# Multi-head latent attention of a two-block transformer: one running sequence of steps over all heads, v computed ahead, the division moved to the output, and the projections of later pairs placed in three of eight steps

## The reference, cut to what matters

```python
up = (c_kv @ kv_w_up).reshape(B, T, MLA_HEADS, QK_NOPE + V_HEAD)   # 16 heads, 64 + 64
k_nope, v_sh = up[..., :QK_NOPE], up[..., QK_NOPE:]
c_q = rmsnorm(h @ q_w_down[j], q_norm_g[j])
q = (c_q @ q_w_up[j]).reshape(B, T, MLA_HEADS, QK_NOPE + QK_ROPE)  # 64 + 32
q_rope = apply_rope(q[..., QK_NOPE:], cos[:, None, :], sin[:, None, :])
...
s = jnp.einsum('bqhd,bkhd->bhqk', qn, k_nope) + jnp.einsum('bqhr,bkr->bhqk', qr, k_rope)
s = s.astype(jnp.float32) * scale
mask = k_chunk[None, :] <= q_chunk[:, None]          # chunks of 64
s = jnp.where(mask[None, None], s, NEG_INF)
p = jax.nn.softmax(s, axis=-1)
return jnp.einsum('bhqk,bkhd->bqhd', p.astype(v.dtype), v)
...
m = o.reshape(B, T, MLA_HEADS * V_HEAD) @ o_w[j]
```

## Time and profile before

| | us |
|---|---|
| median of 3 runs (lowest, highest) | 2600.51 (2596.22, 2605.82) |
| the profiled execution, its own time | 2600.76 |
| its span | 2599.0 |
| TensorE busy in the span | 2374.7 |
| VectorE, ScalarE busy | 1349.9, 970.5 |
| stretch of the phase `heads` | 1093.2 to about 1386 |

### The profile page before, as it was taken

How to read it: one execution, slowest core, us unless ns; L and a number is a source line. 1 busy time by engine, 2 the same in 40 slices (tenths; PEclk the granted TensorE clock), 3 DMA queues, 4 the chain that set the end, 5 groups by cost and what they waited for, 6 DMA issues and landing times.

```text
span 2599.0 us, 38262 instructions
## 1 busy us (share of the span) xinstructions
PE 2374.7 (91%) x14842; PEld 1767.0 (68%) x14842; DVE 1349.9 (52%) x2188; ACT 970.5 (37%) x1544; POOL 60.7 (2%) x84
## 2 busy tenths in 40 slices
PE   5989999968999997799989899999777999999998
PEld 3856666656888884555556688887544787788886
DVE  5566777654646465634442654544555433544443
ACT  4563333324423233434443542323334443422222
POOL 0001111100000000000000000000000000000000
PEclk8999999969999998866778999999866899999999
DMA  3200000012333321100011132322110133232321
GB/s 121 92 28 16 22 14 17 3 70 87 105 97 97 97 83 47 33 11 20 20 54 57 57 105 93 102 90 88 45 41 0 54 96 101 89 105 89 103 85 63
DMA packets 53831, 168.76 MB, mean 65 GB/s; under 512 B 6992, under 2 KB 12240, under 8 KB 53584
## 3 DMA queue, kind: packets, MB, share of 16 engines
q1 hardware_dynamic: 53712, 167.08, 20.2%
HBM read 164.96 MB, written 2.10 MB: 64 GB/s over the span
## 4 chain that ended last, share of the span: by engine, by line
PE 80%; DVE 13%; ACT 3%; issue 2%; DMA 0%; SPq 0%; DVEq 0%; ACTq 0%
PE bank L1496 58%; PE bank L1799 2%; PE bank L1515 2%; PE bank L1565 2%; PE bank L1822 2%; PE bank L1816 2%; PE bank L1802 1%; PE bank L1864 1%; PE bank L1648 1%; DVE rstd L868 1%; PE bank L1629 1%; PE bank L1856 1%; DVE rw_k_inv L1012 1%; PE bank L1878 1%; DVE tmp L897 1%
## 5 line engine op out<-in xcount | busy, mean ns | idle before, releaser
L1496 PE MATMUL bank<-a_hi,w_hi 128*128 128x512 f32 x1488 | 598.2, 402 | 40.2 <-DVE w_lo L862 20.1
L1496 PE MATMUL bank<-a_hi,w_lo 128*128 128x512 f32 x1488 | 583.6, 392 | 0.0
L1496 PE MATMUL bank<-a_lo,w_hi 128*128 128x512 f32 x1488 | 583.0, 392 | 0.0
L862 DVE TENSOR_TENSOR w_lo<-w_raw,w_hi 128x1024 fp32r<-128x1024 f32 (+3 forms) x328 | 361.8, 1106 | 316.5 <-ACT w_hi L484 310.8
L484 ACT ACTIVATE w_hi<-w_raw 128x1024 fp32r<-128x1024 f32 (+3 forms) x328 | 312.0, 956 | 180.6 <-PE bank L1496 179.5
L1496 PEld LDWEIGHTS bank<-a_hi,w_hi 128*128 128x128 f32 x1488 | 281.8, 189 | 120.2 <-issue 38.1
L1496 PEld LDWEIGHTS bank<-a_hi,w_lo 128*128 128x128 f32 x1488 | 282.1, 190 | 62.8 <-issue 6.8
L1496 PEld LDWEIGHTS bank<-a_lo,w_hi 128*128 128x128 f32 x1488 | 281.9, 189 | 59.7
L1496 PE MATMUL bank<-b_hi,w_hi 128*128 128x512 f32 x640 | 260.2, 407 | 21.0 <-DVE b_lo L920 20.3
L1496 PE MATMUL bank<-b_hi,w_lo 128*128 128x512 f32 x640 | 250.8, 392 | 0.0
L1496 PE MATMUL bank<-b_lo,w_hi 128*128 128x512 f32 x640 | 250.6, 392 | 0.0
(11 more groups left out here) (286 smaller groups left out, 3056.5 us busy)
## 6 DMA issues: line engine op xcount, KB each, us to landing
w_raw<-in_f0gu SPq DMA_DIRECT2D x44, 512.0 KB, 3.5
w_raw<-in_f1gu SPq DMA_DIRECT2D x44, 512.0 KB, 3.5
w_raw<-in_f2gu SPq DMA_DIRECT2D x44, 512.0 KB, 3.5
w_raw<-in_f0dn SPq DMA_DIRECT2D x16, 512.0 KB, 3.5
w_raw<-in_f1dn SPq DMA_DIRECT2D x16, 512.0 KB, 3.5
w_raw<-in_mix SPq DMA_DIRECT2D x16, 512.0 KB, 3.5
w_raw<-in_f2dn SPq DMA_DIRECT2D x16, 512.0 KB, 3.5
w_raw<-in_in SPq DMA_DIRECT2D x10, 512.0 KB, 3.5
```

The source lines that it names most:

```text
L862: dve.tensor_tensor(w_lo[r][:, 0:n, :], raw[r][:, 0:n, :], w_hi[r][:, 0:n, :].bitcast(F32), ALU.subtract).then_inc(w_split[r], 1)
L1496: mm = pe.matmul(bank[r][:, :], w[r][:, k, :], a[:, k, :], start=(k == 0 and n == 0), stop=(k == kt - 1 and n == 2))
```

## The change

- **v ahead.** A new phase `vt` of two units of eight tiles computes the values of all 16 heads token-major (`v_all`) straight after `qd`, 48 matmuls of 512 columns in place of the same number spread over the pairs. The sums of the query norm stand between its first four groups. ScalarE copies the eight banks. The transposes of v and their copies are gone.
- **Units by kind.** A pair has three units now (2, 3 and 3 tiles: keys of both heads, queries of both heads, rotary part of both heads with its swapped copy), 24 matmuls, in banks 0 and 1. `kf` and `qf` are double, one set for even and one for odd pairs.
- **Mask in the product.** `kf` and `qf` get four more rows (96 to 99), loaded once, which add the mask within the score matmul; the mask matmul is gone.
- **Running sequence.** The score tiles are numbered g = 0 to 63 through all pairs. In step g TensorE issues the scores of g + 2, the transposes of g, then perhaps weight tiles, then the weighted sum of g - 1. Thirteen weight tiles come ahead of the first step; in each pair, step 1 has three tiles, step 3 two and step 5 three, which belong to units that are one to two pairs ahead. In the last two pairs they run out.
- **Division on the output.** The probabilities stay undivided. The weighted sum holds `prob_t` (128 columns) in the array and streams 64 columns of `v_all`, giving a token-major output in bank 2. VectorE multiplies it by the reciprocal sums once per pair, four transposes turn it into bank 3, and it is split as before.
- Transposed probabilities use banks 6 and 7 in turn, where all used bank 6 before. The loops over pairs are written out.

```diff
+HEAD_TILES = (2, 3, 3)
+HEAD_STEPS = [(u, k) for u in range(3 * PAIRS) for k in range(HEAD_TILES[u % 3])]
+FILL_FIRST = 13
+FILL_BLOCKS = {1: 3, 3: 2, 5: 3}
...
-    out += [("kvd", 3, (8,) * 4), ("qd", 3, (8,) * 4), ("heads", 32, (2, 3, 2, 3)), ("o_w", 8, (8,) * 4)]
+    out += [("kvd", 3, (8,) * 4), ("qd", 3, (8,) * 4), ("vt", 2, (8,) * 4), ("heads", 3 * PAIRS, (3,) * 4),
+            ("o_w", 8, (8,) * 4)]
...
+def head_unit(u):
+    return u % SLOTS, START["heads"][u % SLOTS] + u // SLOTS
...
+        kf = [[at(f"kf{e}{p}", [P, T], R0 + (10 + 2 * e + p) * ROW) for p in range(2)] for e in range(2)]
+        qf = [[at(f"qf{e}{p}", [P, T], (R0, B0)[e] + (14 + p) * ROW) for p in range(2)] for e in range(2)]
+        v_all = [at(f"v_all{n}", [P, TT, T], M0 + 4 * n * ROW) for n in range(2)]
+        prob = [at(f"prob{i}", [P, T], B0 + i * ROW) for i in range(4)]
+        prob_t = [at(f"prob_t{p}", [P, TT, P], B0 + (4 + p) * ROW) for p in range(2)]
+        o_tok = at("o_tok", [P, 8, HEAD], B0 + 6 * ROW)
...
@@ SyncE @@
+            for p in range(2):
+                for e in range(2):
+                    sp.dma_start(kf[e][p][QK:QK + TT, :], dram["mask_k"]).then_inc(const_loaded, 16)
+                sp.dma_start(qf[0][p][QK:QK + TT, :], dram["mask_q"]).then_inc(const_loaded, 16)
...
@@ ScalarE @@
+            def read_v(n):
+                for e, c in enumerate(V_ORDER):
+                    act.wait_ge(*((vt_done, n * (TT - 1) + e + 1) if e < TT - 1 else (unit_done[n], START["vt"][n] + 1)))
+                    act.activation(v_all[n][:, c, :], bank[c][:, :], ACT.Copy)\
+                        .then_inc(vt_free if e < TT - 1 else bank_free[n], 1)
...
+            head_high(0)
+            read_v(0)
             normed("cq", cq)
+            head_high(1)
+            read_v(1)
...
+            for u in range(2, 5):
+                head_high(u)
+            keys(0)
+            head_high(5)
+            queries(0)
+            head_high(6)
+            exp(0)
+            for g in range(8 * PAIRS):
+                i, t = g // 8, g % 8
+                if g + 1 < 8 * PAIRS:
+                    exp(g + 1)
+                if t == 0 and i + 1 < PAIRS:
+                    keys(i + 1)
+                elif t == 1 and i + 1 < PAIRS:
+                    queries(i + 1)
+                turned_copy(g)
+                if t == 2:
+                    head_high(3 * i + 7)
+                elif t == 3:
+                    if i:
+                        output_high(i - 1)
+                    head_high(3 * i + 8)
+                elif t == 5:
+                    head_high(3 * i + 9)
+            output_high(PAIRS - 1)
...
@@ VectorE @@
+            def output_scaled(i):
+                dve.wait_ge(exp_done, 8 * i + 8)
+                dve.reciprocal(stat[:, 32:40], sums_of(i)).then_inc(o_norm_step, 1)
+                dve.wait_ge(o_norm_step, 2 * i + 1)
+                dve.wait_ge(o_done, i + 1)
+                dve.tensor_tensor(o_tok[:, :, :], bank[2][:, :].rearrange("p (t n) -> p t n", t=8),
+                                  stat[:, 32:40].unsqueeze(2).broadcast_to([P, 8, HEAD]), ALU.mult).then_inc(o_norm_step, 1)
...
+            for g in range(8 * PAIRS):
+                i, t = g // 8, g % 8
+                if g + 2 < 8 * PAIRS:
+                    maxima(g + 2)
+                if t == 1 and i:
+                    output_scaled(i - 1)
+                elif t == 2:
+                    head_low(3 * i + 7)
+                elif t == 3:
+                    if i:
+                        output_low(i - 1)
+                    head_low(3 * i + 8)
+                elif t == 4 and i + 1 < PAIRS:
+                    rope_terms(i + 1)
+                elif t == 5:
+                    if i + 1 < PAIRS:
+                        rope_sums(i + 1)
+                    head_low(3 * i + 9)
+            output_scaled(PAIRS - 1)
+            output_low(PAIRS - 1)
             over_units(dve, "o_w", lambda i, r, c: None, low)
...
@@ TensorE @@
+            def values(n):
+                r, c = n, START["vt"][n]
+                pe.wait_ge(w_split[r], c + 1)
+                pe.wait_ge(normed_low, NORMED_AT["ckv"][0] + 2)
+                for e, tok in enumerate(V_ORDER):
+                    if n:
+                        pe.wait_ge(vt_free if e < TT - 1 else bank_free[0],
+                                   e + 1 if e < TT - 1 else START["vt"][0] + 1)
+                    elif tok < 3:
+                        pe.wait_ge(bank_free[tok], START["vt"][tok])
+                    for k in range(2):
+                        for first, (w, a) in enumerate(((w_hi, ckv[0]), (w_lo, ckv[0]), (w_hi, ckv[1]))):
+                            mm = pe.matmul(bank[tok][:, :], a[:, k, cols(tok)],
+                                           w[r][:, TT * k:TT * (k + 1), :].rearrange("p g n -> p (g n)"),
+                                           start=(k == 0 and first == 0), stop=(k == 1 and first == 2))
+                    mm.then_inc(vt_done if e < TT - 1 else unit_done[r], 1)
+                    if n == 0 and e < 3:
+                        sum_squares("n_cq", e)
...
+                if k == 0:
+                    pe.wait_ge(w_split[r], c + 1)
+                    if u >= 2:
+                        before, n = head_unit(u - 2)
+                        pe.wait_ge(bank_free[before], n + 1)
+                for n, (w, a) in enumerate(((w_hi, hi), (w_lo, hi), (w_hi, lo))):
+                    mm = pe.matmul(bank[u % 2][:, :], w[r][:, k, :], a[:, k, :], start=(k == 0 and n == 0),
+                                   stop=(k == HEAD_TILES[u % 3] - 1 and n == 2))
+                if k == HEAD_TILES[u % 3] - 1:
+                    mm.then_inc(unit_done[r], 1)
...
+                pe.matmul(bank[4 + g % 2][:, 0:n], qf[i % 2][p][0:QK + TT, cols(b)], kf[i % 2][p][0:QK + TT, 0:n],
+                          start=True, stop=True).then_inc(s_done, 1)
...
-                    for c in range(TT):
-                        mm = pe.matmul(bank[7][HP[p], c * P:T], v_tok[p][:, c, :], prob_t[p][:, c, c * P:T],
-                                       start=(c == 0), stop=(c == TT - 1), skip_group_check=True)
...
+            def weighted(g):
+                i, t = g // 8, g % 8
+                n = t // 2 + 1
+                if t == 0:
+                    pe.wait_ge(o_norm_step, 2 * i)
+                pe.wait_ge(pt_ready, g + 1)
+                for c in range(n):
+                    mm = pe.matmul(bank[2][:, cols(t, HEAD)], prob_t[g % 2][:, c, :],
+                                   v_all[i // 4][:, c, cols(2 * (i % 4) + t % 2, HEAD)], start=(c == 0),
+                                   stop=(c == n - 1), skip_group_check=True)
+                if t == 7:
+                    mm.then_inc(o_done, 1)
...
+            def turn_output(i):
+                pe.wait_ge(o_norm_step, 2 * i + 2)
+                pe.wait_ge(o_low, i)
+                for b in range(TT):
+                    mm = pe.transpose(bank[3][:, cols(b)], o_tok[:, 2 * b:2 * b + 2, :].rearrange("p t n -> p (t n)"),
+                                      const("ident"))
+                mm.then_inc(ot_done, 1)
...
+            pe.wait_ge(bank_free[1], START["vt"][1] + 1)
+            for step in range(FILL_FIRST):
+                fill(step)
+            pe.wait_ge(shared_rows, 6)
+            pe.wait_ge(const_loaded, 16 * LOADS)
+            scores(0)
+            scores(1)
+            for g in range(8 * PAIRS):
+                i, t = g // 8, g % 8
+                if g + 2 < 8 * PAIRS:
+                    scores(g + 2)
+                turn_prob(g)
+                before = FILL_FIRST + 8 * i + sum(n for at_t, n in FILL_BLOCKS.items() if at_t < t)
+                for step in range(before, before + FILL_BLOCKS.get(t, 0)):
+                    fill(step)
+                if g:
+                    weighted(g - 1)
+                if t == 2 and i:
+                    turn_output(i - 1)
+            weighted(8 * PAIRS - 1)
+            turn_output(PAIRS - 1)
```

More of the change, by code:

```diff
@@ L43 @@
 MLA_HEADS = 16
+PAIRS = MLA_HEADS // 2
 NOPE, ROPE = 64, 32
@@ L107 @@
 KS = {p[0]: p[2] for p in PHASES}
-BY_SLOT = ("heads", "mix")
-STRAIGHT = ("r", "in")
+BY_SLOT = ("mix",)
+STRAIGHT = ("r", "in", "vt", "heads")
 FENCES = ("lora",)
@@ new lines, in rope_terms, with rope_sums @@
+            def rope_terms(i):
+                r, c = head_unit(3 * i + 2)
+                dve.wait_ge(unit_done[r], c + 1)
+                dve.wait_ge(q_rope, 2 * i)
+                rotate(bank[i % 2]).then_inc(bank_free[r], 1)
+            def rope_sums(i):
+                r, c = head_unit(3 * i + 2)
+                dve.wait_ge(rope_term, i + 2)
+                dve.wait_ge(bank_free[r], c + 1)
+                for p in range(2):
+                    rows = slice(HEAD + ROPE * p, HEAD + ROPE * (p + 1))
+                    dve.tensor_tensor(qf[i % 2][p][NOPE:QK, :], rope_a[rows, :], rope_b[rows, 0:T], ALU.add)\
```

(1 more changed line is left out.)

298 lines of the change are left out of this document (141 added, 157 removed).

## The result

| | us |
|---|---|
| median of 4 runs (lowest, highest) | 2459.76 (2457.56, 2461.67) |
| ratio to the kernel before, 95% interval | 0.9457 (0.9437 to 0.9476) |
| the profiled execution, its span | 2461.67, 2459.9 |
| stage from the first unit to `o_w` | 1099.06 to 1246.79 |

The stage took 292.9 us before and takes 147.7 now. It starts 5.8 us later, and 145.2 - 5.8 = 139.4 is the difference of the spans (139.1).

A forecast was written before the change was run, and what follows sets the result against it. TensorE bounds the stage, much of its work at half clock. Step 0 at 1110.1 + 156 (pairs 0 to 5) + 51.4 (last two) + 4.3 waits = 1321.8 against 1386.2, 64 us less: 2536 us, range 2495 to 2566.

The forecast's parts named there:

- v ahead: Before `heads`: v products fill idle TensorE time, but ScalarE's bank copies delay the first unit to 1099.5, 6.2 us later.
- First units: Start of `heads`: 13 weight tiles take 8.9 us, plus 1.7 for a half-clock start; step 0 begins at 1110.1.
- The price of narrow matmuls at full clock: In the pairs: scores 0.42 to 1.06 us, transposes 0.19, weighted sums 0.31; a full pair 22.1 us.
- The clock fell 5.3 us after a dense block: In each pair: the clock falls about 5 us into the longest stretch without dense work, adding 3.9 us, 26.0 a pair.
- the long gap: Stretch of 8.3 us from a pair's third dense block to the next pair's first, claimed to bring the clock down.
- Rows 3 and 4: Profile rows of the kernel before, cited for TensorE's first-pair timeline and the clock's fall at 1107.2 and return at 1127.7.
- Waits: TensorE's waits in the stage: exponentials covered at no cost, 1.3 us for the last output, 3 us small waits; 4.3 us.
- Rival 1: In `heads`: clock stays full throughout because TensorE has no gaps; 106 us less, 2495 us; chance 0.13.
- Rival 2: New weighted sums in the pairs cost their upper bound, 2562 us, chance 0.13; the lower bound gives 2510.
- Rival 4: Every TensorE step waits for ScalarE or VectorE, so slower; 2632 us at 1.5 us idle a step; chance 0.06.

The follow-up runs named there:

- a_mask64: Changed kernel with the mask as a separate matmul over 64 rows instead of inside the score product; 2499.6 us, ratio 0.9618 to the kernel before.
- a_mask1_oneblock: Changed kernel with a separate one-row mask matmul and each pair's eight weight tiles in one block in step 5; 2572.0 us, ratio 0.9898 to the kernel before.
- a_oneblock: Changed kernel with each pair's eight weight tiles in one block in step 5; 2488.0 us, ratio 0.9569 to the kernel before.
- a_mask1: Changed kernel with the mask as a separate matmul over one row behind each score matmul; 2505.0 us, ratio 0.9627 to the kernel before.
- b_mask128: Kernel before with only its mask matmul widened from one row to 128; 2535.0 us, ratio 0.9750 to the kernel before.

## Why the prediction was off

The steps in its own order, from the forecast end of the stage, 1321.8, to the measured 1246.8:

- **v ahead: right.** The first unit was forecast at 1099.5 behind ScalarE's copy of v; it came at 1099.06, with that releaser, behind 3.0 us of idle time (5 forecast).
- **First units: 1.0 us too long.** They took 9.6 us, not 10.6. There was no start at half clock, for which I had added 1.7; the matmuls and a short wait took 0.7 more than forecast.
- **The price of narrow matmuls at full clock: 38.5 us too high.** I summed 6 x 22.1 + 18.7 + 16.6 = 167.9 us of work; it was 1246.8 - 1108.7 - 8.7 = 129.4. The weighted sum was 0.21, not 0.31, because I took it from the mask matmul, the one dear shape in the kernel. The measured value lies nearer to the lower bound, 0.16. Scores were 0.92 and 0.27, not 1.06 and 0.42, which I had read next to one-row masks. Transposes were 0.11, not 0.19, which I had read between weighted sums that hold 64 columns over all 128 rows. There too the weights of the transposes load only as they start (both at 1950.56 and at 1951.73), so an operation over fewer columns may cost its neighbours as well; no run varies the columns. The 64-row scores, to which I put this price in the expectation of `a_mask64`, do not stand beside those transposes. I had treated distances between starts as properties of the instruction, when the neighbours were in them.
- **"The clock fell 5.3 us after a dense block", so that the long gap brings it down in every pair: 39.5 us too much.** It never fell. Rows 3 and 4 were right, but the cause that I read in them, narrow matmuls and transposes, was not: the changed kernel runs 27.3 us of such work at full clock. The rows that I chose left out the wait of 1.45 us at 1105.00, 2.2 us ahead of the fall, and I gave the one-row masks no part in it and priced them only at their own 0.42. The runs showed that the masks set most of the time at half clock (20 to 24 us of a pair with them, 3 to 10 without), but not whether it falls at all in the old order, since it falls without them too. The change takes away the masks and this wait, and puts dense work where waits remain. How the last falls of the old order split between its waits and its transposes of v stays open.
- **Waits: 4.4 us too few** (8.7, not 4.3). The bank of the rotary unit was not in my list.

Together 0.4 + 1.0 + 38.5 + 39.5 - 4.4 = 75.0 us. Rival 1 had the clock right; its stage ended 33.8 us too late, since the same prices were 38.5 too high and the waits 4.4 too few. The Trainium skill ("TensorE: Matmul & The Clock Gate", Why this matters for your kernels) says that a TensorE without idle gaps keeps its full clock, which I set against the busy pair at 0.67. That pair does not settle it, since it had gaps, 1.45 us at 1105.00 the first. The changed kernel, at 1.00 throughout, agrees with it; the first fall of `a_mask1_oneblock`, with 0.23 us of idle time ahead of it, hardly does. Rival 2's lower bound points the right way and does not reach far enough. Rival 4 did not come: the waits are 8.7 us, not 64.

The mask and the order depend on each other. One-row mask to fold is worth 69 us in the old order and 45 in the new; old to new order is worth 95 us with one-row masks (2600 to 2505) and 70 without.

## What to carry to other kernels

Look at the shapes that stand beside each other on TensorE, not only at their number: here a matmul over 64 rows or fewer between wider ones cost about 0.3 us beyond itself, and it endangered the clock. Fold it into the wide product, or widen it to 128 rows, as the mask was here. A wait of one to two microseconds in a stretch without dense work also costs more than itself where the clock falls behind it, as in `a_oneblock`; dense blocks placed over such waits kept it up here. A price read from the distance between two starts holds only with the same neighbours; for a new neighbourhood, give the lower bound the weight.

## What the runs showed of the hardware that I had not expected

- Weight loads come ahead of their matmul between operations over 96, 100 and 128 rows, not into or out of one over 1, 32 or 64 rows (0.43 us early, against 0).
- With excursions the clock fell behind waits that it survived without them (0.98 us in `a_mask1`, 1.88 in the changed kernel), and stayed at half far longer (20 to 24 us of a pair in the kernel before, 3 to 7 at a time in `b_mask128`).
- At 91% busy the granted clock was 0.67 for a pair with one-row masks and its dense work in one piece; without masks or any dense work, and less busy (22.9 of 27.3 us), it stayed at 1.0. The busy share of the records does not tell which it will be. Which amount of idle time brings the clock down stays open: the same wait of 1.43 us for `o_tok` was followed by a fall in four pairs of `a_oneblock`, and by none in two others and in the changed kernel.
